# A hybrid encoder layer with 16 experts: ten expert chunks on chip at the first reload, and six of the first reloads issued by halves

## The reference

```
h = rmsnorm(x) * (1 + sc2) + sh2
aff = softmax(h @ router_w)                     # 512 x 16
gates, idx = top_k(aff.T, 64)                   # each expert takes 64 tokens
hid = silu(h[idx] @ w_gate[e]) * (h[idx] @ w_up[e])   # 1024 x 2048 each
ye = hid @ w_down[e] * gates                    # 2048 x 1024
x = x + gt2 * scatter_add(ye); out = rmsnorm(x) * final_g
```

## Time and profile before

| | |
|---|---|
| median of 3 runs | 1545.53 us (1544.6 to 1546.15) |
| profiled execution, its own time | 1544.05 us |
| its span | 1542.3 us |
| PE busy | 1395.5 us, 90% of the span |
| DVE, ACT busy | 449.9 us (29%), 218.0 us (14%) |
| moved by DMA | 485.52 MB, mean 315 GB/s |
| loads of expert weights | 192 chunks of 2048 KB, 8 of them in halves of 1024 KB |

### The profile page before, as it was taken

One profiled execution on the slowest core, in us unless ns is written; L12 is line 12 of the kernel. 1 busy time (PEld: TensorE's weight loads), 2 busy tenths in 40 slices (PEclk: granted clock), 3 DMA queues, 4 the chain that ended last, 5 costly groups with the idle time before them and its releaser, 6 DMA issues.

```text
span 1542.3 us, 21710 instructions
## 1 busy us (share of the span) xinstructions
PE 1395.5 (90%) x9315; PEld 658.4 (43%) x9315; DVE 449.9 (29%) x813; ACT 218.0 (14%) x444; POOL 39.0 (3%) x45
## 2 busy tenths in 40 slices
PE   5999999999899995999799899799899889889888
PEld 2444544445677553353253253253253243343232
DVE  3799555841246315102102102102101101101102
ACT  2035003322322011110010010010010010010002
POOL 2001230000000000000000000000000000000000
PEclk9999999999899996999999999999999999999999
DMA  9953242182105428999999999999999999999995
GB/s 350 375 178 107 71 98 95 66 212 92 71 4 220 180 109 319 391 427 428 428 428 429 428 429 429 429 428 429 428 428 428 429 428 428 428 428 428 428 426 234
DMA packets 91843, 485.52 MB, mean 315 GB/s; under 512 B 36139, under 2 KB 53629, under 8 KB 62469
## 3 DMA queue, kind: packets, MB, share of 16 engines
q1 hardware_dynamic: 91725, 484.59, 77.3%
q10 hardware_dynamic: 56, 0.01, 0.0%
HBM read 470.93 MB, written 10.50 MB: 312 GB/s over the span
## 4 chain that ended last, share of the span: by engine, by line
PE 65%; DMA 28%; DVE 2%; issue 2%; ACT 1%; POOL 1%; SPq 1%; DVEq 0%; PEldq 0%; POOLq 0%; ACTq 0%
PE psum L1162 15%; DMA arena<-in_exp_w_up_dram 14%; DMA arena<-in_exp_w_gate_dram 13%; PE psum L593 10%; PE psum L1179 9%; PE psum L681 7%; PE psum L1140 4%; PE psum L1072 4%; PE psum L995 2%; DMA arena<-in_ada_w_dram 2%; PE psum L1270 1%; PE psum L1199 1%; PE psum L805 1%; PE psum L728 1%; PE psum L760 1%
## 5 line engine op out<-in xcount | busy, mean ns | idle before, releaser
L1162 PE MATMUL psum<-arena 128*64 128x512 f32 x2048 | 473.3, 619 | 81.3 <-DMA arena<-in_exp_w_up_dram 43.9
L1162 PEld LDWEIGHTS psum<-arena 128*64 128x64 f32 x2048 | 165.2, 142 | 381.7 <-issue 381.2
L1179 PE MATMUL psum<-arena 128*64 128x512 f32 x960 | 208.9, 593 | 6.9 <-issue 5.2
L593 PE MATMUL psum<-arena 128*128 128x512 f32 x336 | 147.4, 599 | 1.4 <-DVE arena L1615 1.4
L1179 PEld LDWEIGHTS psum<-arena 128*64 128x64 f32 x960 | 80.3, 137 | 129.8 <-issue 129.6
L681 PE MATMUL psum<-arena 128*128 128x512 f32 x256 | 122.0, 610 | 0.0
L593 PEld LDWEIGHTS psum<-arena 128*128 128x128 f32 x336 | 63.8, 191 | 82.2 <-issue 79.5
L1992 DVE TENSOR_TENSOR arena<-arena,psum 128x512 f32<-128x512 f32 x32 | 19.9, 682 | 268.6 <-PE psum L1162 268.6
L2006 DVE TENSOR_TENSOR arena<-psum,arena 128x1024 f32<-128x1024 f32 x7 | 8.6, 1225 | 251.8 <-PE psum L1179 251.8
L1517 ACT ACTIVATE arena<-psum,arena 128x128 f32<-128x128 f32 x64 | 24.3, 455 | 333.5 <-PE psum L1140 333.5
L1984 DVE TENSOR_TENSOR arena<-arena,psum 128x512 f32<-128x512 f32 x32 | 19.8, 682 | 168.4 <-ACT arena L1526 168.4
(11 more groups left out here) (282 smaller groups left out, 1103.5 us busy)
## 6 DMA issues: line engine op xcount, KB each, us to landing
arena<-in_exp_w_gate_dram SPq DMA_DIRECT2D x64, 2048.0 KB, 24.3
arena<-in_exp_w_up_dram SPq DMA_DIRECT2D x62, 2048.0 KB, 26.8
arena<-in_exp_w_down_dram SPq DMA_DIRECT2D x60, 2048.0 KB, 26.9
arena<-in_ada_w_dram SPq DMA_DIRECT2D x24, 1024.0 KB, 10.0
arena<-in_w_in_dram SPq DMA_DIRECT2D x16, 1024.0 KB, 5.8
arena<-in_exp_w_down_dram SPq DMA_DIRECT2D x8, 1024.0 KB, 27.0
arena<-in_x_dram SPq DMA_DIRECT2D x2, 2048.0 KB, 8.4
gate_pre<-arena SPq DMA_DIRECT2D x16, 256.0 KB, 6.0
```

The costliest lines, as they stand in the source:

```text
L593: ins = mm(bank(b % 4), by(w_ring[g % 2], KC)[:, k, j * P:(j + 1) * P], by(hT, KC)[:, k, :], start=(k == 0), stop=(k == KC - 1))
L1162: ins = mm(bank(4 * kind + n)[e * 64:(e + 1) * 64, :], by(xeT, KC)[:, k, e * 64:(e + 1) * 64], by(ring[(j + e) % RING], 2)[:, r, n * 512:( ...
L1179: ins = mm(bank(4 + n)[e * 64:(e + 1) * 64, :], by(hidT, FBLK)[:, 4 * kk + b, e * 64:(e + 1) * 64], by(ring[(j + e) % RING], 4)[:, b, n * ...
```

## The change

- Ten chunks are on chip before the first place is reloaded. Chunk 8 is loaded to the place of `x2`, chunk 9 to ring place 7, and chunk 7 to 160 to 176 KB, over DVE's work rows; it therefore waits for the second `rankT_mm`, after which nobody reads them.
- The copy of `x2_first` to `x2` is gone. In pair 0 DVE adds `x2_first` and the result and writes `x2`. For this, pair 0 is written out on PE and DVE, and the loops there run over pairs 1 to 6.
- Places 0 and 1, free after the first gate couple, are reloaded with chunks 16 and 17 instead of 8 and 9. These and the reloads of places 2 to 5 with chunks 10 to 13 are issued by halves. Chunk 14 follows whole, chunk 15 waits for `ring_used` = 10 (chunk 9 used), then chunks 18, 19 and so on as before.
- PE waits where the chunks now land; the semaphores of places 2 to 5 stand 16 higher from the first halved reload on.

```diff
@@ tiles @@
+        first_home = {7: at(160, 16 * KB), 8: x2, 9: ring[7]}
...
@@ SP @@
+            HALVED_LOADS = ((2, 10), (4, 12))
...
-            for j in (6, 7):
-                expert_chunk(0, j)
-            load(x2, x2_first, "late_rows_in")
+            expert_chunk(0, 6)
+            expert_chunk(0, 8, first_home[8], "first_in")
+            expert_chunk(0, 9, first_home[9], "ring7_in")
             sp.wait_ge(sem("router_mm"), TT)
             load(gt2_keep, row(3), "late_rows_in")
-
-            for r in range(2):
-                for e in range(2):
-                    sp.wait_ge(sem("ring_half" if r == 0 else "ring_used"), e + 1)
-                    src = exp_w_up[0, e, 0:2 * P, :].rearrange("(p r) n -> p r n", p=P)
-                    load(by(ring[e], 2)[:, r, :], src[:, r, :], f"w{2 + e}_in" if r == 0 else f"ring{e}_in")
-            for j in range(RING + 2, PER_PAIR + RING):
-                sp.wait_ge(sem("ring_used"), j - RING + 1)
-                expert_chunk(j // PER_PAIR, j % PER_PAIR)
+            sp.wait_ge(sem("rankT_mm"), 2)
+            expert_chunk(0, 7, first_home[7], "first_in")
...
+            for place, j in ((0, 16),) + HALVED_LOADS:
+                for r in range(2):
+                    for e in range(2):
+                        sp.wait_ge(sem("ring_half" if r == 0 else "ring_used"), place + e + 1)
+                        load(*by_halves(place + e, j + e)[r], f"ring{place + e}_in")
+            for j in range(RING + 2 + 2 * len(HALVED_LOADS), PER_PAIR + RING):
+                if j not in (16, 17):
+                    sp.wait_ge(sem("ring_used"), 10 if j == 15 else j - RING + 1)
+                    expert_chunk(j // PER_PAIR, j % PER_PAIR)
...
@@ PE @@
+            def landed(i, j):
+
+                extra = 16 if j % RING in (2, 3, 4, 5) and not (type(i) is int and i == 0 and j < RING) else 0
+                return 48 * i + 16 * (j // RING + 1) + extra
...
-                            elif first and n == 3:
+                            elif first and kind == 0 and kk < 3 and n == 3:
                                 ins.then_inc(sem("ring_half"), 1)
...
-                more_gate(0, kk)
-            with pe.Fori(0, EPAIRS - 1) as i:
+                more_gate(0, kk, True)
+            pair(0, False, True)
+            with pe.Fori(1, EPAIRS - 1) as i:
                 pair(i, False)
...
@@ DVE @@
-                    v.tensor_tensor(x2[:, c:c + 512], x2[:, c:c + 512], bank((6, 4, 5, 7)[n % 4]), ALU.add) \
+                    v.tensor_tensor(x2[:, c:c + 512], before[:, c:c + 512], bank((6, 4, 5, 7)[n % 4]), ALU.add) \
...
-            dve.wait_ge(sem("late_rows_in"), 32)
+            dve.wait_ge(sem("late_rows_in"), 16)
             dve.sem_inc(sem("sum_ready"), 8)
-            with dve.Fori(0, EPAIRS - 1) as i:
+            pair(0, False, x2_first)
+            with dve.Fori(1, EPAIRS - 1) as i:
                 pair(i, False)
```

More of the change, by code:

```diff
@@ L403, in _, with expert_chunk @@
             load(by(wo, KC), w_out[0].rearrange("(k p) n -> p k n", p=P), "wo_in")
-            def expert_chunk(i, j):
+            HALVED_LOADS = ((2, 10), (4, 12))
+            def expert_chunk(i, j, home=None, signal=None):
                 kind, kk, e = j // 8, (j % 8) // 2, j % 2
@@ L410, in expert_chunk @@
                     .rearrange("o (p r) n -> p (o r n)", p=P)
-                load(ring[j % RING], src, f"ring{j % RING}_in")
+                load(ring[j % RING] if home is None else home, src, signal or f"ring{j % RING}_in")
             sp.wait_ge(sem("mod_rows_out"), 64)
@@ L430, in _, with by_halves @@
             sp.wait_ge(sem("norm_sq"), 2 * TT + 1)
-            for j in (6, 7):
-                expert_chunk(0, j)
-            load(x2, x2_first, "late_rows_in")
+            expert_chunk(0, 6)
+            expert_chunk(0, 8, first_home[8], "first_in")
+            expert_chunk(0, 9, first_home[9], "ring7_in")
             sp.wait_ge(sem("router_mm"), TT)
             load(gt2_keep, row(3), "late_rows_in")
-            for r in range(2):
-                for e in range(2):
-                    sp.wait_ge(sem("ring_half" if r == 0 else "ring_used"), e + 1)
-                    src = exp_w_up[0, e, 0:2 * P, :].rearrange("(p r) n -> p r n", p=P)
-                    load(by(ring[e], 2)[:, r, :], src[:, r, :], f"w{2 + e}_in" if r == 0 else f"ring{e}_in")
-            for j in range(RING + 2, PER_PAIR + RING):
-                sp.wait_ge(sem("ring_used"), j - RING + 1)
-                expert_chunk(j // PER_PAIR, j % PER_PAIR)
+            sp.wait_ge(sem("rankT_mm"), 2)
+            expert_chunk(0, 7, first_home[7], "first_in")
+            def by_halves(place, j):
+                kind, kk, e = j // 8, (j % 8) // 2, j % 2
+                w, rows = (exp_w_gate, exp_w_up, exp_w_down)[kind], (2, 2, 4)[kind]
+                src = w[0, e, kk * rows * P:(kk + 1) * rows * P, :].rearrange("(p r) n -> p r n", p=P)
+                return [(by(ring[place], rows)[:, r * rows // 2:(r + 1) * rows // 2, :],
+                         src[:, r * rows // 2:(r + 1) * rows // 2, :]) for r in range(2)]
+            for place, j in ((0, 16),) + HALVED_LOADS:
[7 more added lines that the diff above has]
+                    expert_chunk(j // PER_PAIR, j % PER_PAIR)
             with sp.Fori(1, EPAIRS - 1) as i:
@@ L1144, in gather, with couple, home @@
                         ins.then_inc(sem("xe_mm"), per // 2)
-            def couple(i, j):
+            def landed(i, j):
+                extra = 16 if j % RING in (2, 3, 4, 5) and not (type(i) is int and i == 0 and j < RING) else 0
+                return 48 * i + 16 * (j // RING + 1) + extra
+            def couple(i, j, first=False):
                 for e in range(2):
-                    pe.wait_ge(sem(f"ring{(j + e) % RING}_in"), 48 * i + 16 * ((j + e) // RING + 1))
+                    if first and j + e in (7, 8):
+                        pe.wait_ge(sem("first_in"), 96)
+                    elif first and j + e == 9:
+                        pe.wait_ge(sem("ring7_in"), 16)
+                    else:
+                        pe.wait_ge(sem(f"ring{(j + e) % RING}_in"), landed(i, j + e))
+            def home(j, first):
+                return first_home[j] if first and j in first_home else ring[j % RING]
             def widen(i, kind, kk, first=False):
                 j = 8 * kind + 2 * kk
[L1154 to L1157, removed]
+                couple(i, j, first)
                 for r in range(2):
@@ L1163, in widen @@
                                      by(xeT, KC)[:, k, e * 64:(e + 1) * 64],
-                                     by(ring[(j + e) % RING], 2)[:, r, n * 512:(n + 1) * 512],
+                                     by(home(j + e, first), 2)[:, r, n * 512:(n + 1) * 512],
                                      start=(k == 0), stop=(k == KC - 1))
@@ L1189, in half_narrow @@
                     if not half:
-                        pe.wait_ge(sem(f"ring{2 * kk + e}_in"), 48 * i + 48)
+                        pe.wait_ge(sem(f"ring{2 * kk + e}_in"), landed(i, 16 + 2 * kk + e))
                     elif kk == 3:
@@ L1193, in half_narrow @@
                     else:
-                        pe.wait_ge(sem(f"w{2 + e}_in"), 48)
+                        pe.wait_ge(sem(f"w{2 + e}_in"), 32)
                 pe.wait_ge(sem("hidT_ready"), 4 * i + kk + 1)
@@ L1214, in first_gate, with more_gate, pair @@
                 widen(i, 0, 0, first)
-            def more_gate(i, kk):
+            def more_gate(i, kk, first=False):
                 pe.wait_ge(sem("xe_ready"), 4 * i + kk + 1)
-                widen(i, 0, kk)
-            def pair(i, last):
+                widen(i, 0, kk, first)
+            def pair(i, last, first=False):
                 pe.wait_ge(sem("sum_ready"), 8 * i + 8)
                 for kk in range(4):
-                    widen(i, 1, kk)
+                    widen(i, 1, kk, first)
                 pe.wait_ge(sem("silu_ready"), 4 * i + 4)
@@ L1971, in picks, with pair @@
                     ins.then_inc(sem("pick_ready"), 1)
-            def pair(i, last):
+            def pair(i, last, before=x2):
                 for e in range(2):
@@ L2009, in pair @@
                     dve.wait_ge(sem("put_mm"), 8 * i + n + 1)
-                    v.tensor_tensor(x2[:, c:c + 512], x2[:, c:c + 512], bank((6, 4, 5, 7)[n % 4]), ALU.add) \
+                    v.tensor_tensor(x2[:, c:c + 512], before[:, c:c + 512], bank((6, 4, 5, 7)[n % 4]), ALU.add) \
                         .then_inc(sem("sum_ready"), 1)
             picks(0)
-            dve.wait_ge(sem("late_rows_in"), 32)
+            dve.wait_ge(sem("late_rows_in"), 16)
             dve.sem_inc(sem("sum_ready"), 8)
-            with dve.Fori(0, EPAIRS - 1) as i:
+            pair(0, False, x2_first)
+            with dve.Fori(1, EPAIRS - 1) as i:
                 pair(i, False)
             pair(EPAIRS - 1, True)
-            dve.wait_ge(sem("late_rows_in"), 48)
```

(1 more changed line is left out.)

## The result

The changed kernel takes **1536.18 us** (median of 5 runs, 1535.01 to 1538.91) against 1545.53 before (the median of the five runs compared here, too): 9.35 us less, ratio 0.9940 with a 95% interval of 0.9926 to 0.9954. Forecast were 1537.2, within 1535.0 to 1540.0. Two later comparisons gave ratios of 0.9962 (0.9949 to 0.9975) and 0.9963 (0.9950 to 0.9975), about 5.8 us by these ratios. The trace says which part of this is the change.

What follows compares the result with a forecast made beforehand. The weights' DMA stream bounds the kernel. Chunk 24 landing 9.6 us earlier, less 1.3 us of returning lag, gives 8.3 us: 1545.53 - 8.3 = 1537.2 us, range 1535.0 to 1540.0.

Steps and rivals of the forecast that it cites:

- What bounds the kernel: Expert stage: the weights' DMA stream never rests, 4.894 us a chunk; the end follows when the queue last runs dry.
- the cap: End of pair 0: chunk 24 needs place 0, so it is issued only after narrow 0, at 686.02 us as before.
- rival of 13.3 us: Loads ahead of chunk 24: two more chunks and the closed pause count in full, giving 1532.2 us; chance 0.02.
- rival of time lost by PE in pair 0: Ahead of narrow 0: late chunks 7 to 9 or longer code slow PE; gain 0 to 5 us; chance 0.08.
- rival of half loads that don't overlap: Reloads ahead of chunk 24: each of twelve halves pays 1.75 us; 7.7 us slower, 1553.2 us; chance 0.03.
- The landing of chunk 24: First load of pair 1: lands 7.6 us after issue on a dry queue instead of 17.2, so 9.6 us earlier.
- lag of 1.3 us: Landings behind the full queue: wiped out by the pause, expected back after 687 with more instruction packets; 9.6 - 1.3 = 8.3.
- The pauses: Queue before chunk 24: 3.5 us near 625 gone; new ones of 0.2, 1.7, 1.9, 1.3 us; 5.3 with roundings.
- cap of narrow 1: Chunk 26 in pair 1: needs narrow 1, about 692.8; could flow at 694.6, its turn is at 697.5.
- The copy: Before the reloads: it lay in idle queue time, so taking it away gains nothing directly, only room.
- Written-out pair 0: Pair 0 on PE and DVE: same instructions with constants in place of registers; costs nothing.

Runs made afterwards that it cites:

- e_nine: The changed kernel with nine chunks on chip instead of ten, chunk 9 reloaded by halves; 1539.10 us, ratio 0.9963 to the kernel before.
- e_halves_only: The kernel before with chunks 10 to 13 loaded by halves and nothing else changed; 1542.08 us, ratio 0.9981 to the kernel before.
- e_x2home: The changed kernel with chunk 24 loaded early to the place of x2, not waiting for narrow 0; 1535.85 us, ratio 0.9944 to the kernel before.
- e_written: The kernel before with pair 0 written out on PE and DVE and the copy kept; 1547.82 us, ratio 1.0022 to the kernel before.

## Why the prediction was right

- *What bounds the kernel, and the cap.* As predicted. SP issues chunk 24 at the same moment (77.55 against 77.54 after the head), it lands soon after, and the stream shortens by 8.3 us. The two runs with PE delayed show that it is narrow 0 that decides, and that it did not before. The rival of 13.3 us is out: two chunks and a closed pause are 13.3 us of queue, and 8.3 came out. The rival of time lost by PE in pair 0 is out by the same two issue times. The rival of half loads that don't overlap is out as well: eight of them went through 628 to 648 at 427 GB/s. The Trainium skill ("DMA: Bandwidth & Descriptors", "Anatomy of one DMA — SWDGE (gpsimd) path") gives a fixed cost of about 2.0 us for each DMA and puts most of it down to completion latency; these eight halves show that on this queue it does not add up load by load. The kernel before loads by halves, too: six chunks of the 192, two up chunks of pair 0 and four down chunks of pair 7, and not eight as the table ahead of the prediction has it.
- *The landing of chunk 24.* I took 9.6 us from the earlier trace rows; 9.2 were measured, since it took 8.0 us on the queue and not 7.6. The lag was to come back with more instruction packets, and four more there are after 687 (8 instead of 4). Of the lag of 1.3 us that I added, 0.8 came back by chunk 39 (159.7 against 168.2 after the head, 8.4 us). That the forecast size is met to 0.1 us rests on these two small errors cancelling, 0.4 too much and 0.5 too much taken off again: this much is luck.
- *The pauses.* I listed 0.2, 1.7, 1.9 and 1.3 us and the dips near 649, 656 and 687 are there; the one near 625, forecast as gone, is 0.7 us. I counted the dry time by the sum of transfers, as if all of it were free. e_nine shows that 2.7 us of the 4.9 were not, most of them landings behind the data. For the change itself this did not matter, for what I expected of the experiments it did: three of their sizes were wrong, by 1.2 (e_halves_only), 2.7 (e_nine) and 3.2 us (e_x2home). Of the last, 2.0 us are the cap of narrow 1, which the prediction has in its numbers (694.6 and 697.5) and the expectation left out.
- *The copy.* Costed at nothing, and worth nothing.
- *"Written-out pair 0: Nothing."* This term was probably not nothing. Where nothing else is changed the totals are 0.22% longer (0.11% to 0.32%), with 0.06% for before against itself.
- *The totals.* The forecast went by the stream, and the first comparison gave 9.35 us, two later ones 5.8. As the stream repeats within 0.3 us, the difference between them lies outside it, in head and tail, which the forecast left at nothing. The 5.8 us are 2.5 short of the stream's 8.3, in which the written-out pair is already contained; what it costs outside the stream in e_written (some 2 us, in no place that I can name) would fit, but this is not shown. By the ratio of the later comparisons the forecast would have been 2.5 us too low, 1539.7, still inside its range; that the first median came out within 1.0 us of it is luck in part.
- *The tail.* Not foreseen. The last couple that waits for DMA takes 8.78 us in the first trace of before and 7.09 in that of the change.

The window of that couple, before:

```profile
1481.50:1490.30 8.80, 8.78 (x32) 3.12 (x32) 0.00 (x0) 0.00 (x0) 0.00 (x0) 0.81 1.01 428
```

And with the change:

```profile
1475.22:1482.30 7.08, 7.08 (x32) 2.61 (x32) 0.00 (x0) 0.00 (x0) 0.00 (x0) 1.00 1.00 426
```

The granted clock was 0.81 in the one, a mixture of the levels 1.2 and 2.4 GHz, and 1.00 in the other. Both couples had waited for their weights. Behind the last one the chain goes on with PE's work, so its length goes into the total. In the middle of the stream the next couple waits for its weights anyway; that is argued from the chain, not measured by itself. The second trace of before had the short form, so this is not the change's doing.

## What to carry to other kernels

When a queue that is full to the end sets the time, ask for the first transfer after which it never rests again, and for what releases that transfer: all that is moved ahead of it counts only up to that release. Then look at the next transfer and its release, too: here it stands 2.9 us behind the first and caps what a second step can gain. Count a pause in front of it by the landings, not by the sum of bytes, since part of it may already be used by late transfers. And cut the trace at a point that the change doesn't touch: here the stream repeats within 0.3 us while whole runs scatter by several.

## What the runs showed of the hardware

- Landings fall behind a full queue by 0.2 to 1.5 us at single chunks (in the kernel before 6.2 instead of 4.9 us apart), mostly where an instruction packet of 16 KB goes by, and stay behind until the queue pauses: in the change the stream behind chunk 24 is 1.0 us longer than its data, the sum of such steps. The three largest of its full queue (5.6, 5.3 and 5.2 us, at chunks 21, 26 and 39) have a packet beside them, but not each packet makes a step.
- Half loads of 1 MiB follow each other at 2.4 to 2.5 us, the full rate; a whole chunk on a dry queue lands 7.6 to 8.5 us after its issue.
- Writing out one round of a loop on two engines, with the same instructions in the same order, went with totals longer by 0.22% (0.11% to 0.32%), where the same kernel against itself gave 0.06%.
